# Two fused transformer blocks on one core: PSUM banks given by name, one projection and one bias product issued later, gathering by token tile, waits per half in the scattering

## The chip, the cores and the metric

One Trainium2 chip, one NeuronCore of it. The metric is the device time of one execution in microseconds. "The median" is that of three runs; the profile is of one execution more, whose own time stands beside it.

## What is computed

256 tokens of width 1024 go through two blocks. What the change touches of them, in the reference's own functions:

- Block one mixes latent attention (8 heads, 256 keys) and a Hyena convolution by spectra, then attends to a memory of 256 tokens, then runs a hierarchical mixture of experts. Beside the attention the kernel multiplies block two's conditioning vector with `w_ada_2` (6144 columns in twelve parts of 512, `ada0` to `ada11`).
- Block two normalises and modulates, runs a gated linear recurrence beside an attention with a relative bias (8 heads, causal), and a second mixture of experts.
- A mixture: each of the 256 tokens picks one group of four and two experts of eight in it, so 512 pairs of token and expert; `m = silu(t @ w_gate) * (t @ w_up)`, `y = m @ w_down`, weighted and summed per token. All 32 experts of a block are run.

## The kernel before

**PSUM.** There are eight banks of 128 x 512 float32. Every use of a bank is a stage in one long list (`STAGES`, lines 178 to 209). A stage without bank numbers takes the next banks in turn, a stage with a tuple takes those; lines 210 to 216 number the uses of each bank. `take` makes TensorE wait until the use before of the same bank was released by whoever reads it (`free`), `full` tells the readers that a stage's product is there, `ready` waits for a release. So the numbering decides which older reader a new product waits for.

**Order.** Each engine's program is written out by hand and runs in that order: TensorE (`block.tensor`), ScalarE (`block.scalar`), VectorE (`block.vector`), GpSimd (a few statistics and small loads), SyncE (all large loads, in order, each waiting until its ring slot is vacated). The ring has four slots of 3 MB; unit i goes into slot i mod 4 once unit i-4 is used up (`vacated`, by the table `LAST`). `occupy(stage, j, n)` (line 597) issues n matmuls of 256 columns into a bank that is free and about to be used; their product is overwritten.

**Block one's attention** (loop from line 839, one turn per head h): `ada(h+1)` (16 records of 32 x 512, line 752), transposing the probabilities (`pT`, 831), scores of head h+2 (824), `ada_col(h+1)` (763: one-column products that turn the row into columns), then the product with V (`pv`, 852). After head 2 comes `convolve(0)` (741, 742), after head 5 `z_spectrum(1)` (733), after head 7 `convolve(1)`. ScalarE copies out `ada` (1367) and `pT` (1440), takes the exponentials (1428) and issues the load of the memory tokens from its own queue at head 5 (1444); after the heads it converts weights (477) and squares the memory tokens (1294). VectorE takes the maxima (2007), adds the modulation (1905) and scales the heads (2023).

**A mixture, `moe(b)`** (from line 921): dummies, transposes (`rT`, 612), routing product (`rt`, 934), turned back (`rl`, 940); VectorE picks groups and experts in some 20 short steps; `cnt` (949 to 953) counts pairs by prefix sums; VectorE makes the 0/1 matrix `sel` (2183, 2184, one token tile after the other) and then the weighted one, `selw` (2196 to 2198), clears the tail (2204) and reads two positions into registers; `gx` (972) gathers the tokens for the 512 pairs, eight banks of two token tiles each in a high and a low part; ScalarE copies out the even banks (1566, 1568), VectorE the odd ones (2210, 2212) and then the first windows (2218); `swT` (980) transposes `selw`, VectorE makes it 0/1 (2224). Then come the 32 experts, one step each (997, 1004, 1011, 1017), on six banks counted from that of `yTa`. At the end `start_sum` (1075) opens four sums, `pairs_T` (1111) transposes the results of 64 rows into token form, ScalarE copies the high part (1627), VectorE the low part (2385), and `scatter` (1122, 1123) adds them by token.

In block one the bias product (`bias`, 958) stands between `cnt` and the gathering. It needs two small loads that GpSimd issues after `rt1` (2735, 2736). In block two `gate_row("g2r")` (918) stands there; it needs eight diagonals from ScalarE (1555). Both use the same tensor area as the transposed tokens.

**Block two's attention** (from line 1244): per head `aT` (1249), scores of h+2 (1164, 1165), `beside(h)`, the product with V (1261, 1262). `beside(0)` makes the sums of squares of the first token tile (1214), `beside(1)` those of the second, then the first quarter of an output projection (`wp_lru`). VectorE copies the sums at head 2 (2585) for GpSimd's root; VectorE uses that at head 3. Before it stand the projections `xl`, `aq`, `ak`, `yl`, `av` of the normalised tokens (627 to 629), with `g1r` (918) between `ak` and `yl`.

The stages' banks at the places that the prediction's steps touch, worked out from the list: `yl` takes 6 and 7, used last by `gx` (second) and `ak` (first); block one's experts use the banks from 3 on, block two's from 1 on.

## Time and profile before

| | |
|---|---|
| median of 3 runs | 1034.42 us (1033.56 to 1035.21) |
| the profiled execution, its own time | 1035.14 us |
| its span, first to last instruction | 1033.1 us |
| TensorE | 986.1 us busy (95%), 5320 matmul records |
| VectorE, ScalarE, GpSimd | 583.6, 352.2 and 21.1 us |
| mean granted TensorE clock | 0.988 of full speed |

The profiled execution takes 2.0 us more than its span, and 0.72 us more than the median. A TensorE record's duration overlaps with the next one's, so a busy share near one says that the engine was fed, not that it ran at its peak; the granted clock (1.0 is 2.4 GHz, 0.5 is 1.2 GHz) and what ended an idle stretch have to be read beside it. A float32 matmul leaves two records. "issue" as the releaser means that the profile shows nothing that was waited for; a semaphore of a bank can hide behind it.

### The profile page before, as it was taken

The numbers are of one execution on the slowest core, as the hardware profiler recorded it, in microseconds if no ns is written. First come the engines' busy times: TensorE is split into PE (matmuls) and PEld (weight loads), VectorE is DVE, ScalarE is ACT, GpSimd is POOL, SyncE is SP. The second block draws the span as 40 slices with busy tenths as digits, with TensorE's granted clock in tenths as the row PEclk, the third lists the DMA queues.
The fourth block names the chain that finished last, engine by engine and source line by source line (L and its number), as shares of the span: only waits on it lengthen the run. The fifth ranks groups of instructions, "written<-read, shape, count | busy, mean of one in ns | idle before, by whom it ended". The sixth has DMA issues, their size and how long they took to land.

```text
span 1033.1 us, 14969 instructions
## 1 busy us (share of the span) xinstructions
PE 986.1 (95%) x5320; PEld 593.7 (57%) x5320; DVE 583.6 (56%) x1110; ACT 352.2 (34%) x679; POOL 21.1 (2%) x41
## 2 busy tenths in 40 slices
PE   8999999999999899999999999999899999999985
PEld 7678566977967533443443479876763434434434
DVE  5834437555345546445445475678675655555556
ACT  5654324455445222222222354754441111111113
POOL 1000001000000000000000000000000000000000
PEclk9999999999999899999999999989999999999998
DMA  9263492446407499999999927350619999999931
GB/s 360 120 250 137 195 397 102 163 183 243 166 1 319 180 362 427 424 425 424 428 423 429 397 83 324 141 228 1 245 62 385 423 427 424 426 424 426 424 153 41
DMA packets 28895, 289.04 MB, mean 280 GB/s; under 512 B 3080, under 2 KB 5544, under 8 KB 7728
## 3 DMA queue, kind: packets, MB, share of 16 engines
q1 hardware_dynamic: 25344, 282.04, 66.4%
q0 software_dynamic: 1136, 3.74, 1.1%
q10 hardware_dynamic: 2368, 2.64, 0.8%
q8 instruction: 29, 0.48, 0.2%
q14 instruction: 18, 0.15, 0.0%
HBM read 287.34 MB, written 1.06 MB: 279 GB/s over the span
## 4 chain that ended last, share of the span: by engine, by line
PE 82%; DVE 9%; ACT 3%; DMA 3%; issue 2%; DVEq 0%; SPq 0%; POOL 0%; ACTq 0%; POOLq 0%
PE bank L997 23%; PE bank L1011 11%; PE bank L627 7%; PE bank L628 6%; PE bank L629 6%; PE bank L1017 6%; PE bank L1004 4%; DVE ring_r L484 2%; PE bank L720 2%; PE bank L752 2%; PE bank L972 1%; PE bank L733 1%; PE bank L604 1%; DMA ring<-in_lat 1%; DMA HT<-in_rel_bias 1%
## 5 line engine op out<-in xcount | busy, mean ns | idle before, releaser
L997 PE MATMUL bank<-ring,arena 128*64 128x512 f32 x1040 | 237.5, 598 | 0.2 <-DVE arena L2218 0.2
L2248 DVE TENSOR_REDUCE arena<-bank 128x512 f32 x130 | 83.7, 686 | 117.3 <-PE bank L1017 114.8
L484 DVE TENSOR_TENSOR ring_r<-ring,ring_r 128x1024 fp32r<-128x1024 f32 (+1 forms) x84 | 99.2, 1211 | 85.1 <-ACT ring_r L477 85.1
L997 PEld LDWEIGHTS bank<-ring,arena 128*64 128x64 f32 x1040 | 69.1, 136 | 122.7 <-issue 122.7
L1011 PE MATMUL bank<-ring,arena 128*64 128x512 f32 x520 | 125.8, 604 | 0.5 <-DVE arena L2263 0.3
L477 ACT ACTIVATE ring_r<-ring 128x1024 fp32r<-128x1024 f32 (+1 forms) x84 | 84.8, 1046 | 78.8 <-PE bank L629 77.2
L627 PE MATMUL bank<-HT_r,ring_r 128*128 128x256 f32 x352 | 101.2, 288 | 5.4 <-issue 2.1
L629 PE MATMUL bank<-HT_r,ring_r 128*128 128x256 f32 x352 | 99.6, 283 | 0.0
L1590 ACT ACTIVATE arena<-bank 128x512 f32<-128x512 f32 x64 | 38.3, 598 | 147.6 <-PE bank L997 147.6
L1017 PEld LDWEIGHTS bank<-tab,arena 128*128 128x128 f32 x520 | 55.7, 140 | 54.8 <-issue 49.6
L1017 PE MATMUL bank<-tab,arena 128*128 128x128 f32 x520 | 70.9, 279 | 3.3 <-DVE arena L2277 2.1
L627 PEld LDWEIGHTS bank<-HT_r,ring_r 128*128 128x128 f32 x352 | 67.3, 191 | 8.8 <-issue 8.7
L1584 ACT ACTIVATE arena<-arena 128x128 f32<-128x128 f32 x64 | 19.8, 309 | 152.6 <-DVE arena L2254 152.6
L629 PEld LDWEIGHTS bank<-HT_r,ring_r 128*128 128x128 f32 x352 | 67.4, 191 | 0.0
L628 PE MATMUL bank<-XN_r,ring_r 128*128 128x256 f32 x224 | 63.4, 283 | 0.0
L1011 PEld LDWEIGHTS bank<-ring,arena 128*64 128x64 f32 x520 | 31.7, 136 | 49.7 <-issue 48.3
L1004 PEld LDWEIGHTS bank<-tab,arena 128*128 128x128 f32 x260 | 27.2, 141 | 55.2 <-issue 50.3
L2254 DVE TENSOR_REDUCE arena<-bank 128x256 f32<-128x512 f32 x65 | 44.2, 681 | 12.9 <-PE bank L1004 12.9
L629 PE MATMUL bank<-ring_r,arena_r 128*128 128x512 f32 x128 | 50.6, 396 | 0.0
L2234 DVE COPY arena<-arena 128x512 f32 x62 | 26.5, 427 | 34.6 <-issue 34.6
L1004 PE MATMUL bank<-tab,arena 128*128 128x128 f32 x260 | 42.7, 287 | 2.2 <-ACT arena L1590 1.5
L1596 ACT ACTIVATE arena<-bank 128x512 f32<-128x512 f32 x32 | 19.1, 597 | 72.8 <-PE bank L1011 72.8
(436 smaller groups left out, 1431.5 us busy)
## 6 DMA issues: line engine op xcount, KB each, us to landing
ring<-in_experts SPq DMA_DIRECT2D x64, 2048.0 KB, 14.8
ring<-in_experts SPq DMA_DIRECT2D x64, 1024.0 KB, 11.1
ring<-in_ada SPq DMA_DIRECT2D x12, 2048.0 KB, 10.1
ring<-in_win SPq DMA_DIRECT2D x5, 2048.0 KB, 11.4
ring<-in_hy SPq DMA_DIRECT2D x3, 2048.0 KB, 19.5
ring<-in_mk SPq DMA_DIRECT2D x2, 2048.0 KB, 11.1
ring<-in_mv SPq DMA_DIRECT2D x2, 2048.0 KB, 10.5
ring<-in_wo SPq DMA_DIRECT2D x2, 2048.0 KB, 7.3
```

Of the source, the lines that this page charges most:

```text
L477: nc.scalar.activation(R(h), w, ACT.Copy).then_inc(sem("w_high"), 1)
L484: nc.vector.tensor_tensor(R(w), w, R(h), ALU.subtract).then_inc(sem("w_low"), 1)
L627: mm(ps, R(ah), R(bh), start=first, stop=False)
L628: mm(ps, R(ah), R(bl), start=False, stop=False)
L629: return mm(ps, R(al), R(bh), start=False, stop=last_)
L997: last = mm(gu_bank[g:g + WIN, :], xw[:, k, :], w[:, k * 512:(k + 1) * 512], start=k < 2, stop=k >= KD - 2)
L1004: last = tr(guT_bank[:, c * P:(c + 1) * P], gu_sb[:, c * P:(c + 1) * P], ident)
L1011: last = mm(d_bank[half][64 * f:64 * f + WIN, :], hb[:, f, :], w[:, o:o + 512], start=True, stop=True)
L1017: last = tr(dT_bank[c // 4][:, (c % 4) * P:(c % 4 + 1) * P], d_sb[:, c * P:(c + 1) * P], ident)
L1590: A_(gu_sb, gu_bank[:, :], ACT.Copy).then_inc(sem(f"gu_sb{b}"), 1)
L2248: last = V.reduce_sum(ysT[:, 4 * u:4 * u + 4, bass.ds(s, WIN)], dT_bank[u][:, :].rearrange("p (c g w) -> p c w g", c=4, g=2), AXX)
L2254: return V.reduce_sum(three(gu_sum, 4), guT_bank[:, :].rearrange("p (c g w) -> p c w g", c=4, g=2), AXX)
```

## The change

- **Order in block one's attention**: `ada(3)` moves from the head of turn 2 behind `convolve(0)`; `ada_col(3)`, ScalarE's copy and VectorE's addition for it move into turn 3. One dummy matmul stands between the two parts of `ada_col(1)`, one before the product with V in heads 6 and 7.
- **Banks by name** for both mixtures and the stages between them (`EXPERT`, `SUMS`, tuples). By the list `yl` takes 6 and 7 after `ga` (second) and `gx` (first); block one's experts use banks 5, 6, 7, 0, 1, 2, block two's 4, 5, 6, 7, 0, 1. `yTa1` now follows `gx1` and `bias` in its banks instead of `swT1`.
- **Block one's bias product** moves behind `swT1`, with ScalarE's copy and its small store behind the copies of `swT1`.
- **Gathering**: three banks first take both parts of token tile 0, then of tile 1, with a wait per tile; the other five run as before.
- **Block two's gate row** moves before the counts, its diagonals on ScalarE before the two exponentials; numbers of dummies change.
- **Scattering** waits for one half of 512 columns at a time and, but for the last part, runs by halves.
- **Block two's attention**: both token tiles' sums of squares move behind the first quarter of the projection in head 1; two dummies stand in head 0.

```diff
--- before.py
+++ after.py
@@ -189,16 +189,22 @@
 STAGES += [("ada8", 1), ("mo", 4), ("ada9", 1)]
 
 
+EXPERT = {1: (5, 6, 7, 0), 2: (4, 5, 6, 7)}
+SUMS = {1: (1, 2, 3, 4), 2: (0, 1, 2, 3)}
+
+
 def _moe_stages(b):
     one = b == 1
-    return [(f"rT{b}", 4)] + [("adac8", 1)] * one + [(f"rt{b}", 1), (f"rl{b}", 1, (3,))] + [("adac9", 1)] * one \
-        + [(f"cnt{b}", 1)] + [("bias", 1)] * one + [("g2r", 2, (5, 6))] * (b == 2) + [(f"gx{b}", 8), (f"swT{b}", 2, (3, 4))] \
-        + [(f"yTa{b}", 4), (f"sct{b}", 4), (f"yTb{b}", 4)]
+    return [(f"rT{b}", 4, *(() if one else ((3, 4, 5, 6),)))] + [("adac8", 1)] * one + [(f"rt{b}", 1), (f"rl{b}", 1, ((3,), (5,))[b - 1])] + [("adac9", 1)] * one \
+        + [(f"cnt{b}", 1)] + [("g2r", 2, (0, 1))] * (b == 2) + [(f"gx{b}", 8, ((3, 4, 5, 6, 7, 0, 1, 2), (4, 5, 6, 7, 0, 1, 2, 3))[b - 1])] \
+        + [(f"swT{b}", 2, ((3, 4), (6, 7))[b - 1])] + [("bias", 1, (0,))] * one \
+        + [(f"yTa{b}", 4, EXPERT[b]), (f"sct{b}", 4, SUMS[b]), (f"yTb{b}", 4, EXPERT[b])]
 
 
 STAGES += _moe_stages(1)
-STAGES += [("ada10", 1), ("ada11", 1)]
-STAGES += [("uT", 4), ("xl", 2), ("adac10", 1), ("adac11", 1), ("aq", 2), ("ga", 2), ("gx", 2), ("ak", 2), ("g1r", 2)]
+STAGES += [("ada10", 1, (1,)), ("ada11", 1, (2,))]
+STAGES += [("uT", 4, (3, 4, 5, 6)), ("xl", 2, (7, 0)), ("adac10", 1, (1,)), ("adac11", 1, (2,)), ("aq", 2, (3, 4)),
+           ("ga", 2, (5, 6)), ("gx", 2, (7, 0)), ("ak", 2, (1, 2)), ("g1r", 2, (3, 4))]
 STAGES += [("yl", 2, (6, 7)), ("av", 2, (4, 5)), ("as0", 1, (0,)), ("as1", 1, (1,))]
 for _h in range(H1):
     STAGES += [(f"aT{_h}", 1, (2,))] + ([(f"as{_h + 2}", 1, (_h % 2,))] if _h + 2 < H1 else [])
@@ -762,6 +768,8 @@
                     for c in range(4):
                         last = mm(ps[:, 4 * a + c:4 * a + c + 1], ada_sum(n)[:, c * P:(c + 1) * P], ones[:, 0:1],
                                   start=True, stop=True)
+                    if a + 1 < len(parts):
+                        mm(ps[:, 256:512], ident, T("iota")[:, 0:256], start=True, stop=True)
                 full(last, f"adac{i}")
 
             pe.wait_ge(sem("tab"), 32)
@@ -837,14 +845,18 @@
             for t in range(TT):
                 ready(pe, "uv", t)
             for h in range(H1):
-                if h < 6:
+                if h < 6 and h != 2:
                     ada(h + 1)
+                if h == 3:
+                    ada_col(3)
                 ready(pe, f"sc{h}")
                 probs_T(f"pT{h}", prob[:, h % 2])
                 if h + 2 < H1:
                     mla_scores(h + 2)
-                if h < 6:
+                if h < 6 and h != 2:
                     ada_col(h + 1)
+                if h >= 6:
+                    occupy(f"pv{h}", 0, 1)
                 ready(pe, f"pT{h}")
                 ps = take(pe, f"pv{h}")
                 for t in range(TT):
@@ -854,6 +866,7 @@
                 full(last, f"pv{h}")
                 if h == 2:
                     convolve(0)
+                    ada(3)
                 if h == 5:
                     z_spectrum(1)
             convolve(1)
@@ -920,7 +933,7 @@
 
             def moe(b):
                 if b == 2:
-                    occupy("rT2", 0, 17)
+                    occupy("rT2", 0, 18)
                 transposed(f"rT{b}", XN, KD, f"xn_r{b}")
                 if b == 1:
                     ada_col(8)
@@ -942,7 +955,9 @@
                 full(last, f"rl{b}")
                 if b == 1:
                     ada_col(9)
-                occupy(f"cnt{b}", 0, 10 if b == 2 else 8)
+                occupy(f"cnt{b}", 0, 6 if b == 2 else 8)
+                if b == 2:
+                    gate_row("g2r", diag2, "diag2")
 
                 pe.wait_ge(sem("hot"), b)
                 ps = take(pe, f"cnt{b}")
@@ -951,27 +966,26 @@
                 mm(ps[:, NE:2 * NE], ones, M12[:, 0, :], start=False, stop=True)
                 mm(ps[:, 2 * NE:3 * NE], ones, M12[:, 0, :], start=True, stop=False)
                 full(mm(ps[:, 2 * NE:3 * NE], ones, M12[:, 1, :], start=False, stop=True), f"cnt{b}")
-                if b == 1:
-                    pe.wait_ge(sem("onehot"), 32)
-                    pe.wait_ge(sem("mask_row"), 1)
-                    ps = take(pe, "bias")
-                    full(mm(ps[0:H1, :], relb[0:BUCKETS + 1, :], oneh[0:BUCKETS + 1, :], start=True, stop=True), "bias")
-
-                if b == 2:
-                    occupy("g2r", 0, 3)
-                    gate_row("g2r", diag2, "diag2")
-                occupy(f"gx{b}", 0, 4 if b == 2 else 6)
-
-                pe.wait_ge(sem(f"sel{b}"), TT)
-                pe.wait_ge(sem("xn_low"), TT * b)
-                for k in range(KD):
-                    ps = take(pe, f"gx{b}", k)
+                occupy(f"gx{b}", 0, 6)
+
+                def gather(k, t):
+
+                    for i, x in enumerate((xn_high, xn_low)):
+                        last = mm(gx[k][:, :], R(x[:, t, k * P:(k + 1) * P]), R(sel[:, t, :]),
+                                  start=t + i == 0, stop=t + i == TT)
+                    if t:
+                        full(last, f"gx{b}", k)
+
+                gx = [take(pe, f"gx{b}", k) for k in range(3)]
+                for t in range(TT):
+                    pe.wait_ge(sem(f"sel{b}"), t + 1)
+                    pe.wait_ge(sem("xn_low"), TT * (b - 1) + t + 1)
+                    for k in range(3):
+                        gather(k, t)
+                for k in range(3, KD):
+                    gx.append(take(pe, f"gx{b}", k))
                     for t in range(TT):
-
-                        for i, x in enumerate((xn_high, xn_low)):
-                            last = mm(ps[:, :], R(x[:, t, k * P:(k + 1) * P]), R(sel[:, t, :]),
-                                      start=t + i == 0, stop=t + i == TT)
-                    full(last, f"gx{b}", k)
+                        gather(k, t)
                 pe.wait_ge(sem(f"selw{b}"), TT)
                 for j in range(2):
                     ps = take(pe, f"swT{b}", j)
@@ -980,7 +994,12 @@
                             last = tr(ps[:, a * S + t * P:a * S + (t + 1) * P],
                                       selw[:, t, (2 * j + a) * P:(2 * j + a + 1) * P], ident)
                     full(last, f"swT{b}", j)
-                occupy(f"yTa{b}", 0, 2)
+                if b == 1:
+                    pe.wait_ge(sem("onehot"), 32)
+                    pe.wait_ge(sem("mask_row"), 1)
+                    ps = take(pe, "bias")
+                    full(mm(ps[0:H1, :], relb[0:BUCKETS + 1, :], oneh[0:BUCKETS + 1, :], start=True, stop=True), "bias")
+                occupy(f"yTa{b}", 0, 2 if b == 2 else 1)
                 for k in range(KD):
                     ready(pe, f"gx{b}", k)
                 if b == 2:
@@ -1040,6 +1059,8 @@
                         if isinstance(e, int) and e == 1:
                             for j in range(2):
                                 ready(pe, f"swT{b}", j)
+                            if b == 1:
+                                ready(pe, "bias")
 
                         before = 16 * (NE // RING) * (b - 1)
                         rounds = 16 * ((e - 1) // RING + 1) if isinstance(e, int) else \
@@ -1114,16 +1135,16 @@
                 def scatter(pt):
 
                     stage = (f"yTa{b}", f"yTb{b}")[pt // 2]
-                    for half in range(2):
+                    end = pt == NPAIR // P - 1
+                    for q in range(4):
+                        t, half = (q // 2, q % 2) if end else (q % 2, q // 2)
                         ready(pe, stage, 2 * (pt % 2) + half)
-                    for t in range(TT):
-                        for half in range(2):
-                            tok, cols = slice(t * P, (t + 1) * P), slice(half * 512, (half + 1) * 512)
-                            mm(acc[2 * t + half][:, :], R(swT[:, pt, tok]), R(ytok[:, pt, cols]), start=False, stop=False)
-                            last = mm(acc[2 * t + half][:, :], R(swT[:, pt, tok]), R(ytok_low[:, pt, cols]),
-                                      start=False, stop=pt == NPAIR // P - 1)
-                            if pt == NPAIR // P - 1:
-                                full(last, f"sct{b}", 2 * t + half)
+                        tok, cols = slice(t * P, (t + 1) * P), slice(half * 512, (half + 1) * 512)
+                        mm(acc[2 * t + half][:, :], R(swT[:, pt, tok]), R(ytok[:, pt, cols]), start=False, stop=False)
+                        last = mm(acc[2 * t + half][:, :], R(swT[:, pt, tok]), R(ytok_low[:, pt, cols]),
+                                  start=False, stop=end)
+                        if end:
+                            full(last, f"sct{b}", 2 * t + half)
 
                 pairs_T(f"yTa{b}", range(0, 4))
                 scatter(0)
@@ -1219,14 +1240,12 @@
             def beside(h):
 
                 if h == 0:
-                    pe.wait_ge(sem("squared"), 4)
-                    lss = take(pe, "lss")
-                    token_sums(lss, sq, range(4), (0,))
-                    wp_ps["lss"] = lss
+                    occupy("ap0", 0, 2)
                 elif h == 1:
-                    full(token_sums(wp_ps["lss"], sq, range(4), (1,)), "lss")
                     pe.wait_ge(sem("lo_low"), 1)
                     wp_lru(0, 0)
+                    pe.wait_ge(sem("squared"), 4)
+                    full(token_sums(take(pe, "lss"), sq, range(4)), "lss")
                 elif h == 2:
                     wp_lru(0, 1)
                 elif h in (4, 5):
@@ -1432,7 +1451,9 @@
             mla_exp(0)
             mla_exp(1)
             for h in range(H1):
-                if h < 6:
+                if h == 3:
+                    ada_evac(3)
+                if h < 6 and h != 2:
                     ada_evac(h + 1)
                 ps = got(act, f"pT{h}")
                 if h >= 2:
@@ -1546,20 +1567,16 @@
                 ps = got(act, f"rt{b}")
                 free(A_(turned, ps[:, 0:S], ACT.Copy), f"rt{b}")
                 A_(R(xn_high[:, 1, :]), XN[:, 1, :], ACT.Copy).then_inc(sem("xn_high"), 1)
+                if b == 2:
+                    for k in range(KD):
+                        last = A_(diag2[:, k, :], ident, ACT.Copy, scale=mod[:, 40 + k:41 + k])
+                    last.then_inc(sem("diag2"), 1)
                 act.wait_ge(sem("e_diff"), b)
                 A_(ex2, m2, ACT.Exp).then_inc(sem("e_exp"), 1)
                 act.wait_ge(sem("g_diff"), b)
                 A_(gex, cand4, ACT.Exp).then_inc(sem("g_exp"), 1)
                 if b == 2:
-                    for k in range(KD):
-                        last = A_(diag2[:, k, :], ident, ACT.Copy, scale=mod[:, 40 + k:41 + k])
-                    last.then_inc(sem("diag2"), 1)
                     copies("g2r", [g2row[:, 0:512], g2row[:, 512:1024]])
-                if b == 1:
-                    ps = got(act, "bias")
-                    free(A_(brow[0:H1, :], ps[0:H1, :], ACT.Copy), "bias")
-                    ready(act, "bias")
-                    act.dma_start(bias_rows, brow[0:H1, :]).then_inc(sem("bias_out"), 16)
                 for k in range(0, KD, 2):
                     ps = got(act, f"gx{b}", k)
                     if shift is None:
@@ -1574,6 +1591,11 @@
                                   accum_out=pair_w[:, 2 * j + a:2 * j + a + 1])
                     last.then_inc(sem("x_high"), 1)
 
+                if b == 1:
+                    ps = got(act, "bias")
+                    free(A_(brow[0:H1, :], ps[0:H1, :], ACT.Copy), "bias")
+                    ready(act, "bias")
+                    act.dma_start(bias_rows, brow[0:H1, :]).then_inc(sem("bias_out"), 16)
                 for j in range(2):
                     ready(act, f"swT{b}", j)
                 gu_bank, guT_bank, d_bank, dT_bank = expert_banks(b)
@@ -2017,7 +2039,9 @@
                     mla_max(h + 2)
                 ready(dve, f"sc{h}")
                 link(V.reciprocal(rinv[:, h, :], rsum[:, h, :]))
-                if h < 6:
+                if h == 3:
+                    modulation(3)
+                if h < 6 and h != 2:
                     modulation(h + 1)
                 ps = got(dve, f"pv{h}")
                 free(V.tensor_tensor(AO[:, :, h * VD:(h + 1) * VD], three(ps[:, 0:TT * VD], TT),
```

## Rows read from the trace of the kernel before

**Rows 1.** The page: the chain that ended last, by engine, and the expert loop's costliest group.
```profile
PE 82%; DVE 9%; ACT 3%; DMA 3%; issue 2%; DVEq 0%; SPq 0%; POOL 0%; ACTq 0%; POOLq 0%
...
L997 PE MATMUL bank<-ring,arena 128*64 128x512 f32 x1040 | 237.5, 598 | 0.2 <-DVE arena L2218 0.2
```

**Rows 2.** Timeline of TensorE in block one's attention: start us, us, engine, line, operation, count.
```profile
123.73 2.89 PE L752 MATMUL bank<-ring,cm 128*32 128x512 f32 x16 [1.89 <-DMA ring<-in_ada]
...
130.31 1.08 PE L741 MATMUL bank<-arena 128*128 128x512 f32 x2
...
142.36 1.92 PE L752 MATMUL bank<-ring,cm 128*32 128x512 f32 x16
...
147.40 1.92 PE L752 MATMUL bank<-ring,cm 128*32 128x512 f32 x16
```

**Rows 3.** Timeline of ScalarE and VectorE beside it, heads three to seven.
```profile
141.60 0.16 DVE L1905 TENSOR_TENSOR mod<-bank,col 128x4 f32<-128x4 f32 x1
...
164.54 1.06 ACT L1294 ACTIVATE arena<-XN 128x1024 f32<-128x1024 f32 x1
```

**Rows 4.** DMA queues, 150 to 160 us: ScalarE's queue, and that load's time to landing.
```profile
q10 hardware_dynamic: 131, 0.54, 13.9%
...
XN<-in_mem ACTq DMA_DIRECT2D x1, 1024.0 KB, 12.8
```

**Rows 5.** Timeline of TensorE from block one's counts to its first expert.
```profile
339.22 1.54 PE L958 MATMUL bank<-HT 33*8 33x512 f32 x2 [2.54 <-DMA HT<-in_rel_bias]
...
345.61 8.01 PE L972 MATMUL bank<-arena_r 128*128 128x512 f32 x32
...
356.06 1.13 PE L604 MATMUL bank<-tab 128*128 128x256 f32 x4 [1.57 <-DVE arena_r L2224]
357.12 3.65 PE L997 MATMUL bank<-ring,arena 128*64 128x512 f32 x16
```

**Rows 6.** Stretches: length, TensorE busy (instructions), granted clock, DMA share, GB/s.
```profile
339.22:345.61 6.39, 6.39 (x14) 0.53 1.00 424
...
686.25:695.41 9.16, 9.16 (x33) 0.63 0.67 284
```

**Rows 7.** Timeline of VectorE after block one's counts.
```profile
339.31 0.75 DVE L2184 SCALAR_TENSOR_TENSOR arena_r<-tab,arena,arena_r 128x512 fp32r<-128x512 f32 x1
...
346.30 0.48 DVE L2204 MEMSET arena<- 128x512 f32 x1
```

**Rows 8.** The same stage in block two: VectorE, and TensorE's first expert.
```profile
763.04 0.48 DVE L2204 MEMSET arena<- 128x512 f32 x1 [0.17 <-DVE arena L2198]
...
764.20 2.97 DVE L2212 TENSOR_SCALAR arena<-bank,mod 128x512 f32<-128x512 f32 x4 [0.67 <-issue]
...
768.09 3.65 PE L997 MATMUL bank<-ring,arena 128*64 128x512 f32 x16 [0.21 <-DVE arena L2218]
```

**Rows 9.** Timeline of the scattering, block one (block two shows the same pattern).
```profile
589.65 2.73 DVE L2385 SCALAR_TENSOR_TENSOR arena_r<-bank,arena,arena_r 128x512 fp32r<-128x512 f32 x4 [1.77 <-ACT arena_r L1627]
591.21 0.47 PE L1122 MATMUL bank<-arena_r 128*128 128x512 f32 x1 [1.14 <-DVE arena_r L2385]
```

**Rows 10.** Timeline at the start of the stage `yl`: VectorE and TensorE.
```profile
656.48 1.41 DVE L1824 COPY arena<-bank 128x256 f32<-128x256 f32 x4
...
657.33 0.36 PE L627 MATMUL bank<-HT_r,ring_r 128*128 128x256 f32 x1 [1.88 <-issue]
```

**Rows 11.** Timeline of TensorE in block two's attention, heads zero and one.
```profile
685.30 1.02 PE L1214 MATMUL bank<-tab,arena 128*128 128x1 f32 x8 [0.71 <-ACT arena L1360]
...
695.41 0.65 PE L1261 MATMUL bank<-arena 128*64 128x256 f32 x2
```

**Rows 12.** Timeline of block two's routing: ScalarE's copies and TensorE's dummies.
```profile
732.49 7.50 PE L604 MATMUL bank<-tab 128*128 128x256 f32 x34
...
746.60 1.05 ACT L1548 ACTIVATE arena_r<-XN 128x1024 fp32r<-128x1024 f32 x1
...
752.65 2.43 ACT L1555 ACTIVATE HT<-tab,mod 128x128 f32<-128x128 f32 x8
```

## The prediction

> **What bounds the kernel now.** I read the chain of waits first. TensorE carries 82% of it, VectorE 9% [rows 1], so a microsecond counts only where TensorE stands still, runs at its lower clock, or does something it need not. Then I asked of the largest stage, the 64 expert steps, whether there is anything to gain or lose: over 1040 records TensorE was idle 0.2 us in all before them [rows 1]. The experts' loop is fed without a hole, and its instructions stay as they are. What can move is the seams between stages. For each seam that the diff touches I read TensorE's timeline (its idle time and what ended it), the granted clock of the stretch behind it, and the timelines of ScalarE and VectorE beside it, because the seam is worth only what the next-latest engine leaves of it.
>
> **The change part by part.** Negative is faster.
>
> *Block one's heads.* After head 1 TensorE waits 1.89 us for the weights of `ada(3)`, up to 123.73 [rows 2]; head 2 therefore runs from 121.84 to 130.31, where `convolve(0)` starts: 8.47 us. An undisturbed turn with the same work takes 147.40 - 142.36 = 5.04 us [rows 2]. The difference, 3.43 us, is the wait and the lower clock behind it (the record group behind the wait takes 2.89 us against 1.92 for the same 16 records [rows 2]). Once `ada(3)` stands behind `convolve(0)`, some 7 us later, its weights have long landed. Added: a dummy in `ada_col(1)`. 17 dummies take 7.50 us [rows 12], so one takes 0.44 and two 0.88; this one lies on TensorE's path: +0.44. The later `ada_col(3)` shares its bank with `pv3`, and VectorE frees that only after head 5's maximum: its addition takes 0.16 us at 141.60 in the turn shown [rows 3], right behind the maximum, while TensorE would go on with `pv` at once; I put the wait at the addition and the reciprocal before it, two steps of 0.16 and their hand-over: +0.4 (none at best, 0.6 at worst). The dummies of heads 6 and 7 stand between a transpose and the product that needs ScalarE's copy of it, a gap that hides 0.44; uncovered they would cost 0.9 together. TensorE thus saves 2.6 us.
> But the next stage starts from VectorE, which needs the memory tokens' squares, and ScalarE begins those at 164.54 [rows 3], just when the load lands: issued at head 5, it takes 12.8 us to land [rows 4]. If the load's time stays, it lands 2.6 us earlier with its issue; if the bytes before it set its end, hardly at all. By 160 us its queue had moved only 0.54 MB of 1.05 [rows 4], so both limits play a part. The ends are -2.6 and -0.5; I take -1.9, nearer to the first because the row is a transfer that advanced beside the others all the time. The later `ada_col(3)` also holds back the next large load on SyncE's queue by some 6 us, behind two others under way: hidden, or 1 us if not.
> The Trainium skill ("DMA: Bandwidth & Descriptors", section on queues, rings and completion order) says that each DMA engine takes turns packet by packet between the queues that have work. Taken alone that gives the load a share from its issue on, and so the whole -2.6; the 0.54 MB agree that it got one.
>
> *Block one's bias product and gathering.* The counts end 2.54 us before 339.22, at 336.68; TensorE then waits for the small load of the bias, and the six dummies and the bias behind it run at a granted 0.53 until 345.61, where the gathering starts [rows 5, 6]. VectorE had the first tile's `sel` at 339.31 + 0.75 = 340.06 [rows 7]. After: dummies 336.7 to 339.3, an idle 0.8 us, gathering from 340.1; its 32 records take at most the 8.0 us of before [rows 5] and end by 348.1. By token tile, TensorE works six records on the first tile, 1.5 us, until the second tile is there at 341.3.
> What is late next is VectorE. It is busy with `selw` up to its memset at 346.30, unchanged [rows 7]. From there I take block two's rows: evacuation 1.16 us after the memset began, four of them in 2.97 us, the first expert 3.89 us after the first evacuation began [rows 8]. So 346.30 + 1.16 + 3.89 = 351.35. Against 357.12 [rows 5]: -5.8. TensorE has to be ready by then: `swT1` needs a bank of the first odd evacuation (348.2), the bias one of the third (347.5 + 3 x 0.74 = 349.7); with the bias at 0.8 us and one dummy it is done at 351.0, with the bias at its 1.54 us of the lower clock [rows 5] at 351.7. That bounds the term at -5.4. Before, the dummies waited 1.57 us for VectorE's copy of `swT1` [rows 5]; by the new banks nothing waits for it before the first step's end. The bias's store on ScalarE's queue, 0.6 us of copy and as much of issue, now delays nothing but ScalarE's first copy of an expert, which is due only after 16 records of 3.65 us.
>
> *Block two's gathering.* The same edits find VectorE already last: it begins its evacuations 1.16 us after the memset whatever TensorE does, and the first expert waits for it [rows 8]. The gate row moves into the time of the four dummies taken from before the counts; its diagonals (2.43 us) can start at 746.60 + 1.05 [rows 12] and end at 750.1, the two products at 751.9, the counts are due at 752.4. So 0. If the diagonals were late the counts would be: up to 1 us. The 18th dummy before the transposes stands where VectorE's normalisation is last; uncovered, 0.44.
>
> *Scattering.* Before the first `scatter` TensorE waits 1.14 us for VectorE's second half; one low part takes 2.73 / 4 = 0.68 us [rows 9]. Waiting for the first half only saves that 0.7. The last part follows VectorE as closely, and I put 0.2 on it, an estimate (none at least, another 0.7 at most): -0.9 in each block, -1.8 in all.
>
> *Banks before `yl`.* TensorE stands 1.88 us before `yl` with no releaser named; VectorE's copies of `ak` begin at 656.48, and 0.7 us later the first of its banks is free, when `yl` starts at 657.33 [rows 10]. With banks 6 and 7 after `ga` and `gx`, both read by ScalarE long before, nothing holds it: -1.9. The converted weights behind it follow TensorE's own use, so they move along.
>
> *Block two's heads 0 and 1.* Before: 0.71 us idle, then 0.95 us of one-column products up to 686.25 [rows 11]; the stretch from there to head 1's product with V at 695.41 takes 9.16 us at a mean granted clock of 0.63 [rows 6, 11]. At full clock the same records take 9.16 x 0.63 = 5.8 us: -3.4. The idle time and first sums are replaced by two dummies (0.88 us instead of 1.66: -0.8), and those sums come back in head 1 (+0.95). Together -3.2 if the clock stays up, +0.2 if it does not. VectorE reads the sums only at head 2. I take -3.2: the idle time that preceded the fall is filled.
>
> **Sum:** -1.9 - 5.8 + 0 - 1.8 - 1.9 - 3.2 = -14.6. The profiled execution, 1035.1 us, becomes 1020.5; it lies 0.7 above the median, so the median of 1034.4 becomes 1019.8.
>
> **Rivals.**
> *The clock falls all the same.* In the two seams where it fell before, idle stretches of 0.8 to 1.0 us and one-column products remain, now side by side with others. Against: 1.57 us idle before 356.06 [rows 5] were followed by none, as the next 16 records took the 3.65 us that they take in block two [rows 5, 8]. In block two's heads that costs 3.4, before block one's experts up to 0.4 by TensorE's readiness and up to 1 more by a late eighth bank: 1023.2 to 1024.6. Chance 0.2.
> *The memory load is bound by bytes.* The first term shrinks to -0.5: 1021.2. For: half of it was outstanding at 160. By the page's rule of turns it would not be. Chance 0.12.
> *VectorE's chain takes over in block two's heads.* It is 56% busy over the span, has a dozen short steps in each head, and then of the 3.2 only the part before head 1 stays, 0.8: 1022.2. Against: the lower clock held TensorE, not VectorE, which so has time in hand [rows 6]. Chance 0.06.
> *The banks are not what held `yl`.* The profile names no releaser [rows 10]; if it was the converted weights, the change does nothing there: 1021.7. Chance 0.03.
> *Slower: the experts' banks.* If the new pairing of the six banks lengthened each of the 64 steps, 0.23 us a step would eat all 14.6; at 0.3 us, half a record, it is 64 x 0.3 = 19.2 on 1019.8, so 1039.0. Against: the two blocks use different banks already and TensorE is held 0.2 us in both together [rows 1]. Chance 0.02.
>
> **The numbers.** All terms as summed: 0.57, at 1019.8, by itself 1017.5 to 1021.5. The range must take in the clock and the load, alone and together, and below it terms that I bounded from above (the hole of 1 us that dummies leave): 1015.5 to 1025.5. About 0.2% of this kernel's time, 2 us, is what a measurement can tell from no change. For that 12.6 us of the sum would have to fail: faster 0.96, the same 0.02, slower 0.02.
>
> **What the profile after would show.** `ada(3)` behind `convolve(0)` with no DMA named before it, head 2 in about 5 us or less, clock 1.0; the squares of the memory at 162 to 164. The gathering about 3.5 us after the counts, 0.8 to 1 us idle before it, block one's first expert 5.0 to 5.2 us after the memset. No idle time before `yl`. Clock 1.0 through heads 0 and 1. First `scatter` 0.5 us after its transposes. The same length of an expert's step as before, in both blocks. Wrong would be: an expert step of another length, a stretch at 0.5 in one of the seams, or VectorE or a DMA named before the stage behind a seam with the same idle time as before.

## The result, and the profile after

The changed kernel took 1020.77 us (median of four runs, 1019.63 to 1022.08), the kernel before 1034.58 beside it (1033.56 to 1035.21): a ratio of 0.9868, 95% interval [0.9851, 0.9885]. The forecast was 1019.8, in a range from 1015.5 to 1025.5. The profiled execution has a span of 1017.6 us against 1033.1, 15.5 less; the medians differ by 13.8. That gap of 1.7 us turned out to be the most instructive part of the case, below.

The timeline of TensorE in block one's attention, after (columns as in [rows 2]):

```profile
122.06 0.61 PE L839 MATMUL bank<-tab,arena 128*128 128x128 f32 x4
...
124.30 1.08 PE L747 MATMUL bank<-arena 128*128 128x512 f32 x2
...
131.32 3.64 PE L758 MATMUL bank<-ring,cm 128*32 128x512 f32 x32
...
138.44 1.08 PE L864 MATMUL bank<-arena 128*128 128x64 f32 x8 [0.36 <-DVE mod L1927]
...
149.43 1.08 PE L739 MATMUL bank<-arena 128*128 128x512 f32 x2
```

Head 2 begins with its transposes and no wait, and `convolve(0)` starts at 124.30 instead of 130.31. `ada(3)` and `ada(4)` stand together behind it, 32 records without a wait. The only new wait is 0.36 us for VectorE's addition, in the bank that `ada_col(3)` shares with `pv3`. `z_spectrum(1)` starts at 149.43, before at 152.35. The memory tokens' load takes 13.0 us, and the stage behind it moves along (the timelines of ScalarE and TensorE):

```profile
161.81 1.06 ACT L1313 ACTIVATE arena<-XN 128x1024 f32<-128x1024 f32 x1
...
172.82 0.36 PE L633 MATMUL bank<-HT_r,ring_r 128*128 128x256 f32 x1 [1.01 <-DVE arena_r L1870]
```

The squares start 2.73 us earlier than in [rows 3]. ScalarE's own weight conversion in front of them ended at about the same moment in both kernels (at 164.63 before, at 161.71 after), so the load was not the only thing that they could have waited for. The large loads ahead of that one moved as well (SyncE's queue, issues):

```profile
143.64 5.37 SPq L539 DMA_DIRECT2D ring<-in_mv x2
```

The first of these two was issued at 146.56 before. The seam before block one's experts, against [rows 5]:

```profile
333.74 2.84 PE L610 MATMUL bank<-tab 128*128 128x256 f32 x12
337.54 7.54 PE L974 MATMUL bank<-arena_r 128*128 128x512 f32 x32 [0.97 <-DVE arena_r L2208]
344.92 0.60 PE L994 MATMUL bank<-tab,arena 128*128 128x128 f32 x4
345.67 0.66 PE L994 MATMUL bank<-tab,arena 128*128 128x128 f32 x4
347.08 1.01 PE L1001 MATMUL bank<-HT 33*8 33x512 f32 x2 [0.74 <-DVE arena L2234]
348.02 0.70 PE L610 MATMUL bank<-tab 128*128 128x256 f32 x2
348.65 3.65 PE L1016 MATMUL bank<-ring,arena 128*64 128x512 f32 x16
```

The wait of 2.54 us for the bias's input is gone, the 12 records of dummies take 2.84 us instead of 5.49, and the gathering starts 3.8 us after the counts' end. VectorE's memset is at 343.52 and the first expert 5.13 us behind it. In block two, against [rows 8], VectorE is again what the first expert waits for:

```profile
751.80 1.03 PE L610 MATMUL bank<-tab 128*128 128x256 f32 x4
753.64 0.65 PE L1016 MATMUL bank<-ring,arena 128*64 128x512 f32 x2 [0.81 <-DVE arena L2242]
```

TensorE stands 0.81 us there where it stood 0.21 before, and the first expert comes 14.45 us earlier than before, as much as the counts ahead of it (14.49). The start of scattering and of `yl`, against [rows 9, 10]:

```profile
582.25 0.50 PE L1143 MATMUL bank<-arena_r 128*128 128x512 f32 x1 [0.40 <-DVE arena_r L2409]
```

```profile
644.29 1.88 PE L931 MATMUL bank<-arena,tab 128*128 128x512 f32 x4
645.61 0.68 PE L633 MATMUL bank<-HT_r,ring_r 128*128 128x256 f32 x1
```

`yl`'s first record now follows the gate row with no idle time. And block two's heads 0 and 1, against [rows 11]:

```profile
673.13 1.13 PE L610 MATMUL bank<-tab 128*128 128x256 f32 x4
674.19 0.65 PE L1280 MATMUL bank<-arena 128*64 128x256 f32 x2
...
679.16 1.84 PE L1235 MATMUL bank<-tab,arena 128*128 128x1 f32 x16
680.93 0.65 PE L1280 MATMUL bank<-arena 128*64 128x256 f32 x2
```

Their stretch, with its granted clock (third number after the length: PEclk), against [rows 6]:

```profile
674.19:680.93 6.74, 6.74 (x40) 5.41 (x39) 4.67 (x11) 3.80 (x10) 0.00 (x0) 1.00 0.99 421
```

6.74 us at full clock in place of 9.16 at 0.63. The experts' group has the same duration as in [rows 1], to the digit:

```profile
L1016 PE MATMUL bank<-ring,arena 128*64 128x512 f32 x1040 | 237.5, 598 | 1.0 <-DVE arena L2242 0.8
```

**One table for all that follows.** I took the same ten landmarks of TensorE from the profiled execution of every kernel. A column is the length of a stretch, in us, and below the first line the difference from the changed kernel. A: start to `z_spectrum(1)`. B: to block one's counts. C: to its first expert. D: its experts, to `start_sum`. E: scattering, to `xl`. F: to block two's first transposed probabilities. G: to head 1's product with V. H: to the transposes for block two's routing. I: to its first expert. K: to the end.

| kernel | A | B | C | D | E | F | G | H | I | K | span |
|---|---|---|---|---|---|---|---|---|---|---|---|
| changed | 149.43 | 183.17 | 16.05 | 226.45 | 27.41 | 69.35 | 9.07 | 45.58 | 27.13 | 263.96 | 1017.6 |
| before | +2.92 | -0.14 | +5.69 | -0.26 | +1.09 | +2.09 | +3.09 | +0.01 | -0.04 | +1.05 | 1033.1 |
| u1 | +1.65 | +0.20 | +0.02 | -0.27 | +0.03 | -0.01 | 0.00 | +3.16 | -0.02 | +0.04 | 1022.4 |
| u2 | +0.23 | +0.12 | +3.80 | -0.27 | +0.07 | +0.02 | 0.00 | +0.03 | -0.03 | +0.23 | 1021.8 |
| u3 | +0.19 | +0.11 | +0.02 | -0.27 | -0.01 | -0.01 | 0.00 | +1.59 | -0.03 | +0.01 | 1019.2 |
| u4 | +0.19 | -0.01 | +0.01 | -0.27 | +0.07 | +3.12 | 0.00 | +1.55 | -0.03 | -0.03 | 1022.2 |
| u5 | +2.09 | +0.10 | +0.02 | -0.27 | +0.01 | -0.01 | +4.46 | +0.13 | -0.04 | +0.01 | 1024.1 |
| u6 | +2.80 | -0.08 | +0.02 | -0.27 | -0.01 | +0.03 | -0.21 | +3.11 | -0.02 | +0.03 | 1023.0 |
| u9 | +1.76 | +0.11 | +0.02 | -0.27 | -0.01 | +0.02 | -0.01 | 0.00 | -0.03 | +0.01 | 1019.2 |
| u7 | -0.14 | +0.09 | +0.02 | +1.41 | +1.10 | 0.00 | 0.00 | +0.02 | -0.04 | +1.14 | 1021.2 |
| u10 | +1.83 | +0.18 | +0.34 | -0.26 | +0.02 | 0.00 | 0.00 | +0.06 | -0.03 | -0.04 | 1019.7 |
| u8 | -0.29 | +0.19 | +0.02 | -0.26 | -0.01 | +0.01 | 0.00 | +0.05 | -0.04 | +0.03 | 1017.3 |
| n1 | +0.15 | +0.37 | -1.18 | -0.27 | +0.03 | +0.03 | 0.00 | +0.03 | -1.47 | +0.01 | 1015.3 |
| n3 | +0.10 | +0.69 | -1.21 | -0.27 | +0.02 | 0.00 | 0.00 | +1.57 | -1.45 | +0.05 | 1017.1 |

Most cells from C on that no edit touches agree within 0.1 us, those of A and B within some 0.3, so a seam can be read to a tenth or three where the total can't: the four or five runs of one kernel spread over 1 to 4 us. The ratios below carry little of the argument: of the twelve variants only n1 and n3 have an interval that lies clear of the changed kernel's, and the ten from u1 to u10 overlap with it. So what a part is worth rests on the traces, one execution of each kernel. The record adds the mean clock of every timed run, to 0.001, which is about 1 us of lost clock on this kernel; the four of the changed kernel have 0.996 or 0.997. The cells that are large without an edit (A of u1, u5, u6, u9, u10; D of u7; H of u1, u3, u4, u6, n3) are a finding of their own, told last; B of n1 and n3 is the memory tokens' load, which landed later there. D is 0.27 longer in the changed kernel than in all others, before included: block one's last expert waited 0.20 us for its weights in that one execution.

```profile
564.63 0.65 PE L1016 MATMUL bank<-ring,arena 128*64 128x512 f32 x2 [0.20 <-DMA ring<-in_experts]
```

### The profile page after: what moved, and what is told of

The parts are those of the page before. It is cut to its first block and busy times, and to the rows that moved or that the text cites. A ratio compares the mean times of both kernels' runs of the same rounds, so it can differ in the third digit from the quotient of the medians.

```text
span 1017.6 us, 14965 instructions
## 1 busy us (share of the span) xinstructions
PE 978.0 (96%) x5320; PEld 588.6 (58%) x5320; DVE 583.0 (57%) x1110; ACT 352.4 (35%) x679; POOL 21.1 (2%) x41
## 3 DMA queue, kind: packets, MB, share of 16 engines
HBM read 287.34 MB, written 1.06 MB: 283 GB/s over the span
```

## The experiments

All twelve start from the changed kernel. Those of one group ran on one chip beside the kernel before, and each ratio is to that.

### Group one: the parts put back one by one (before: 1035.37 us)

**u1.** Back in head 2: `ada(3)`, its copy on ScalarE and its addition on VectorE.
```
-                if h < 6 and h != 2:
+                if h < 6:
                     ada(h + 1)
-                if h == 3:
-                    ada_col(3)
...
                     convolve(0)
-                    ada(3)
...
```


> The changed kernel with ada(3), its copy and its addition back at head 2, all else as changed. Theory: TensorE waits about 1.9 us for the weights of ada(3) again, its clock falls behind the wait, head 2 takes some 8.5 us up to convolve(0) instead of 5.1, and mk starts about 2.7 us later: 1023.5 (1022.7 if the wait comes back but the clock stays up). Rival, that the gain there came from the dummies: no change, 1020.8. Second rival, that the memory load's end is set by the bytes before it: the load, issued about 2.9 us later, lands at nearly the same time, and the total is 1021.3 or less.

1022.38 us (1021.05 to 1024.37), ratio 0.9866 [0.9849, 0.9883]. No wait for weights came back; something else stood in its place:

```profile
117.38 3.61 PE L758 MATMUL bank<-ring,cm 128*32 128x512 f32 x16
...
124.10 1.92 PE L758 MATMUL bank<-ring,cm 128*32 128x512 f32 x16
...
129.04 1.08 PE L747 MATMUL bank<-arena 128*128 128x512 f32 x2
```

```profile
117.38:124.10 6.72, 6.72 (x42) 0.75 0.98 380
```

In head 1, with no idle time ahead of them, the 16 records of `ada(2)` took 3.61 us instead of 1.92, at a mean clock of 0.75. TensorE thus came to `ada(3)` at 124.10, after the moment at which it had been released in [rows 2] (123.73), and found its weights. The slow stretch and the wait are substitutes: the 1.65 us in A is the slow stretch (the same records are 1.5 to 1.7 us longer in three other kernels), and the order itself cost nothing in this execution. So the gain of part one depends on what head 1 did: in the profiled pair 2.9 us, here none. None of the three expectations named this mechanism, though the ratio, 0.9866 against 0.9868, is the one that the first rival (no change) gives. The median is 1.6 above that of the changed kernel, in another comparison and inside the spread. One timed run had a clock of 0.997, as high as the changed kernel's best, and a span of 1019.1 us against 1017.6 and 1018.0 there: a cost of 1.1 to 1.5 us without the lower clock, as the wait would make; that run has no trace.

**u2.** The bias product in front of the gathering again, in bank 2, with ScalarE's copy and store; two dummies stand before the first expert again instead of one.
```
+                if b == 1:
+                    pe.wait_ge(sem("onehot"), 32)
+                    pe.wait_ge(sem("mask_row"), 1)
+                    ps = take(pe, "bias")
+                    full(mm(ps[0:H1, :], relb[0:BUCKETS + 1, :], oneh[0:BUCKETS + 1, :], start=True, stop=True), "bias")
                 occupy(f"gx{b}", 0, 6)
...
-                occupy(f"yTa{b}", 0, 2 if b == 2 else 1)
+                occupy(f"yTa{b}", 0, 2)
...
```


> The changed kernel with block one's bias product (and ScalarE's copy and store of it) back in front of the gathering, which stays by token tile. Theory: the product's late input and the lower clock behind it come back, block one's first expert starts 5.5 to 5.8 us later, 1026.4. Rival, that gathering by token tile brought part of it: only 4.5 us or less come back, 1025.3 or less. Block two is untouched under both.

1022.97 us (1021.92 to 1023.91), ratio 0.9873 [0.9855, 0.9891].

```profile
336.70 1.64 PE L973 MATMUL bank<-HT 33*8 33x512 f32 x2 [2.44 <-DMA HT<-in_rel_bias]
338.27 5.49 PE L610 MATMUL bank<-tab 128*128 128x256 f32 x12
343.20 7.90 PE L979 MATMUL bank<-arena_r 128*128 128x512 f32 x32
350.93 1.03 PE L999 MATMUL bank<-tab,arena 128*128 128x128 f32 x8
351.80 1.03 PE L610 MATMUL bank<-tab 128*128 128x256 f32 x4
352.80 1.08 PE L1016 MATMUL bank<-ring,arena 128*64 128x512 f32 x4
```

Wait and lower clock came back in full: the gathering starts 5.31 us later relative to the counts. But the first expert does so by 3.80 only. The other 1.9 of the 5.69 us lay behind the gathering before. There the dummies waited 1.57 us for the bank of the turned weights, with VectorE's copy of them named as releaser [rows 5]; u2, with the named banks, has no such wait. From the start of VectorE's last evacuation to the first expert it is 3.46 us before and 1.67 in u2, while from the gathering's start to that evacuation it is 8.05 and 7.93. So the order of gathering can be worth 0.1 of it and the banks the rest, and the rival had the size and not the reason. No run puts the old banks back by themselves.

**u3.** The gathering slice by slice, each waiting for both token tiles.
```
-                gx = [take(pe, f"gx{b}", k) for k in range(3)]
-                for t in range(TT):
-                    pe.wait_ge(sem(f"sel{b}"), t + 1)
...
-                    for k in range(3):
-                        gather(k, t)
-                for k in range(3, KD):
+                gx = []
+                pe.wait_ge(sem(f"sel{b}"), TT)
...
+                for k in range(KD):
...
```


> The changed kernel with the gathering slice by slice, each waiting for both token tiles, in both blocks. Theory, VectorE's evacuations set the first expert: gathering starts 1.2 us later, but the first expert only 0.7 us later in block one (the bias product still has to fit in) and 0 to 0.2 in block two: 1021.6. Rival, that TensorE sets it: 1.2 us in each block, 1023.2. Second rival, wholly hidden: 1020.8.

1021.37 us (1020.94 to 1022.23), ratio 0.9862 [0.9845, 0.9879]. The gathering starts 1.0 us later in both blocks, and both first experts are where they were: 0.02 and -0.03 in C and I.

```profile
338.83 7.55 PE L974 MATMUL bank<-arena_r 128*128 128x512 f32 x32 [1.96 <-DVE arena_r L2205]
...
347.39 1.01 PE L998 MATMUL bank<-HT 33*8 33x512 f32 x2
```

The bias product had waited 0.74 us for a bank; now it does not. Gathering by token tile is worth nothing here.

**u4.** `ak` in the two banks that `yl` takes next.
```
-           ("ga", 2, (5, 6)), ("gx", 2, (7, 0)), ("ak", 2, (1, 2)), ("g1r", 2, (3, 4))]
+           ("ga", 2, (5, 6)), ("gx", 2, (7, 0)), ("ak", 2, (6, 7)), ("g1r", 2, (3, 4))]
```


> The changed kernel with ak's products in banks 6 and 7, which yl takes right behind them, all other banks as changed. Theory, banks held yl: TensorE stands about 1.9 us before yl again until VectorE has read ak's first bank, and the end is 2.1 us later, 1022.9. Rival, that the wait was for the converted weights: no idle time, 1020.8.

1024.71 us (1024.23 to 1025.84), ratio 0.9896 [0.9879, 0.9913].

```profile
649.05 0.36 PE L633 MATMUL bank<-HT_r,ring_r 128*128 128x256 f32 x1 [2.55 <-DVE arena L1846]
```

The wait is back, and here the profile names its releaser, VectorE's copies of `ak`. It is longer than the 1.88 us of [rows 10], and F is 3.12 us longer instead of 2.1. Banks held `yl`: shown. The ratio's interval still overlaps with the changed kernel's, but every run of u4 (1024.23 and more) is slower than every run of that (up to 1022.08).

### Group two: block two's heads, and scattering (before: 1034.14 us)

**u5.** The first tile's sums in head 0 instead of the dummies, the second's in head 1, as before the change.
```
                 if h == 0:
-                    occupy("ap0", 0, 2)
+                    pe.wait_ge(sem("squared"), 4)
+                    lss = take(pe, "lss")
+                    token_sums(lss, sq, range(4), (0,))
...
                 elif h == 1:
+                    full(token_sums(wp_ps["lss"], sq, range(4), (1,)), "lss")
...
-                    full(token_sums(take(pe, "lss"), sq, range(4)), "lss")
```


> The changed kernel with the sums of the squares back in heads 0 and 1 of block two and without the two dummies of head 0. Theory: about 0.7 us of idle time and 0.95 us of one-column products come back, the clock falls behind them, and the stretch up to head 1's product with V takes about 9.2 us at a mean of 0.6: 3.2 us later, 1024.0. Rival, the clock has nothing to do with it: 0.2 us, 1021.0.

1024.64 us (1024.43 to 1026.12), ratio 0.9898 [0.9868, 0.9927]. The rows of the seam, and its clock:

```profile
675.85 1.02 PE L1235 MATMUL bank<-tab,arena 128*128 128x1 f32 x8 [0.71 <-ACT arena L1381]
676.80 0.65 PE L1282 MATMUL bank<-arena 128*64 128x256 f32 x2
...
680.20 1.86 PE L1235 MATMUL bank<-tab,arena 128*128 128x1 f32 x8
```

```profile
676.80:687.33 10.53, 10.53 (x33) 0.53 0.59 249
```

4.46 us, 1.4 more than in the kernel before: the lower level began earlier (the transposes at 677.79 already take 0.90 instead of 0.55) and lasted through the stretch. All four timed runs have a clock of 0.991 or 0.992.

**u6.** Only the two dummies left out.
```
                 if h == 0:
-                    occupy("ap0", 0, 2)
+                    pass
```


> The changed kernel without the two dummies of head 0 (the sums stay in head 1). Theory A, idle time makes the clock fall: 1.6 us of idle before the first product with V, then the lower clock, about 3 us later, 1023.8. Theory B, it was the one-column products that made it fall: the clock stays at 1.0, nothing is later, 1020.8.

1022.15 us (1020.67 to 1024.99), ratio 0.9869 [0.9837, 0.9901].

```profile
676.48 0.62 PE L1280 MATMUL bank<-arena 128*64 128x256 f32 x2 [0.80 <-ACT arena L1379]
```

```profile
676.48:683.21 6.73, 6.73 (x40) 1.00 0.96 408
683.21:691.29 8.08, 8.08 (x24) 0.59 0.05 19
```

TensorE stood 0.80 us idle, half of what I had expected but more than the 0.71 before the change, and the clock stayed up through heads 0 and 1: theory A falls for an idle time of this length, and the dummies buy nothing there (G is even 0.21 shorter). But in head 2, behind the 16 records of one-column products that now end head 1, the clock fell: 3.11 us in H.

**u9.** Both: the two dummies, and behind them the sums as in u5.
```
                 if h == 0:
                     occupy("ap0", 0, 2)
+                    pe.wait_ge(sem("squared"), 4)
+                    lss = take(pe, "lss")
+                    token_sums(lss, sq, range(4), (0,))
...
```


> The changed kernel with two dummies in head 0 and behind them the sums of the first token tile, those of the second in head 1 as before. Theory A (idle time decides): the clock stays at 1.0, head 0 is up to 0.9 us longer and head 1 some 0.9 us shorter, 1020.9. Theory B (one-column products decide): the clock falls, 1023.9.

1021.29 us (1019.52 to 1021.67), ratio 0.9860 [0.9829, 0.9891]. Clock 1.0 from 676.61 to 682.55, G unchanged. So theory B doesn't hold alone either. Of four arrangements only idle time and one-column products together, as before the change and in u5, brought the lower clock inside this seam; either of the change's two edits would have kept it out in these executions. Each arrangement has one trace, but the timed runs agree: clocks of 0.995 to 0.997 in u9, and 0.995 or 0.996 in three of u6's four, against u5's 0.991 and 0.992.

**u7.** Each `scatter` waits for both halves and goes by token tile.
```
-                    for q in range(4):
-                        t, half = (q // 2, q % 2) if end else (q % 2, q // 2)
-                        ready(pe, stage, 2 * (pt % 2) + half)
+                    for half in range(2):
+                        ready(pe, stage, 2 * (pt % 2) + half)
+                    for q in range(4):
+                        t, half = q // 2, q % 2
```


> The changed kernel with each scatter waiting for both halves and taking token tile by token tile, in both blocks. Theory: the wait before the first scatter grows from 0.4 to 1.1 us, and the last part is some 0.4 us later: 1.1 us in each block, 1022.9. Rival, only the first scatter counts: 0.7 in each, 1022.2.

1023.57 us (1022.07 to 1024.40), ratio 0.9887 [0.9856, 0.9918]. The first part waits as in [rows 9]:

```profile
584.37 0.47 PE L1144 MATMUL bank<-arena_r 128*128 128x512 f32 x1 [1.15 <-DVE arena_r L2410]
```

E and K are 1.10 and 1.14 longer: 0.74 and 0.75 at the first part, 0.36 and 0.39 at the last. The theory's 1.1 a block is shown.

### Group three: dummies, and a better version (before: 1034.89 us)

**u10.** No dummies before block one's gathering.
```
-                occupy(f"gx{b}", 0, 6)
+                occupy(f"gx{b}", 0, 6 if b == 2 else 0)
```


> The changed kernel without the six dummies before block one's gathering: TensorE stands about 3.8 us there instead of 1. Theory: the clock falls and the gathering runs part of its time at the lower level, 2 to 4 us of which VectorE does not hide: 1023 to 1025. Rival, the clock stays up or the fall is hidden behind VectorE: 1020.8.

1021.56 us (1020.13 to 1021.95), ratio 0.9864 [0.9848, 0.9879].

```profile
339.55 9.07 PE L974 MATMUL bank<-arena_r 128*128 128x512 f32 x32 [3.64 <-DVE arena_r L2208]
348.46 1.03 PE L994 MATMUL bank<-tab,arena 128*128 128x128 f32 x8
```

The clock did fall: the same 32 records take 9.07 us instead of 7.54. Of these 1.53 us only 0.34 reach the first expert; VectorE's evacuations hide the rest. The theory had the fall right and the uncovered part wrong.

**u8.** Without the dummies in `ada_col(1)` and in heads 6 and 7.
```
-                    if a + 1 < len(parts):
-                        mm(ps[:, 256:512], ident, T("iota")[:, 0:256], start=True, stop=True)
...
-                if h >= 6:
-                    occupy(f"pv{h}", 0, 1)
```


> The changed kernel without the dummy in ada_col(1) and those of block one's heads 6 and 7. Theory: the first costs its own 0.4 us and buys nothing, the others lie in a wait for ScalarE: 0.4 us earlier, 1020.4, clock unchanged. Rival, they keep the clock up: a stretch at the lower level behind head 1 or in heads 6 and 7, 1 to 2 us later, 1022.3.

1022.32 us (1019.28 to 1023.58), ratio 0.9879 [0.9862, 0.9896]. A is 0.29 shorter than in the changed kernel and about 0.5 shorter than in u2 to u4; the clock stayed up in this profiled execution, whose span of 1017.3 is below the changed kernel's. But it was the exception. The other three timed runs have clocks of 0.994, 0.992 and 0.993, below all four of the changed kernel, and spans of 1019.3 to 1021.6 us, and the median is the rival's number (1022.3). This speaks for the rival, that the dummies make a fall of the clock rarer; where those three runs lost their clock no trace shows, and the interval overlaps with the changed kernel's, so it is not shown.

**n1.** ScalarE evacuates six gathered slices as TensorE completes them, VectorE two.
```
-                for k in range(0, KD, 2):
+                for k in (0, 1, 2, 3, 4, 6):
...
-                for k in range(1, KD, 2):
+                for k in (5, 7):
```


> The changed kernel with ScalarE evacuating six of the eight gathered slices as TensorE completes them (0 to 4 and 6) and VectorE only slices 5 and 7, in both blocks. Theory, VectorE's four evacuations are what is last before the first expert: it starts 1.2 us earlier in block one and 1.5 in block two, 1018.1. Rival, TensorE's transposes and the bias product are nearly as late: half of that, 1019.5. Second rival, block one's experts wait for their weights at the loop's end by as much as they start earlier: 1019.3.

1017.49 us (1016.70 to 1018.89), ratio 0.9832 [0.9819, 0.9846]: faster than both kernels, since the interval lies below the changed kernel's [0.9851, 0.9885] against the same kernel before. The theory's 1.2 and 1.5 us measured 1.18 and 1.47.

```profile
345.39 1.41 DVE L2234 TENSOR_SCALAR arena<-bank,col 128x512 f32<-128x512 f32 x2 [0.87 <-issue]
```

```profile
345.44 1.03 PE L994 MATMUL bank<-tab,arena 128*128 128x128 f32 x8
346.40 1.02 PE L1001 MATMUL bank<-HT 33*8 33x512 f32 x2
347.36 0.70 PE L610 MATMUL bank<-tab 128*128 128x256 f32 x2
347.99 1.51 PE L1016 MATMUL bank<-ring,arena 128*64 128x512 f32 x6
```

TensorE now runs from the gathering into the experts with no hole.

**n3.** The edits of n1 (not shown again), and the memory tokens' load issued ahead of head 7's exponentials.
```
+                if h + 2 == H1 - 1:
+                    got(act, f"sc{h + 2}")
+                    act.dma_start(XN, A["mem"].rearrange("(t p) d -> p t d", p=P)).then_inc(sem("mem_in"), 16)
                 if h + 2 < H1:
                     mla_exp(h + 2)
-                if h + 2 == H1 - 1:
-                    act.dma_start(XN, A["mem"].rearrange("(t p) d -> p t d", p=P)).then_inc(sem("mem_in"), 16)
```


> The same, and ScalarE issues the memory tokens' load as soon as head 7's scores are done (the last reader of the buffer), ahead of the exponentials instead of behind them. Theory, the load takes the same 13 us from its issue: its squares and mk start 0.9 us earlier, 1017.2. Rival, the bytes before it set its end, or convolve(1) becomes the last: mk moves less than 0.3 us, 1018.0.

1018.19 us (1017.46 to 1019.89), ratio 0.9834 [0.9821, 0.9847]. The load was issued at 148.00 instead of 148.94 in n1, took 14.5 us instead of 13.3, and its squares began no earlier (n3's timeline, then n1's):

```profile
162.54 1.06 ACT L1313 ACTIVATE arena<-XN 128x1024 f32<-128x1024 f32 x1 [0.72 <-DMA XN<-in_mem]
```

```profile
162.28 1.06 ACT L1313 ACTIVATE arena<-XN 128x1024 f32<-128x1024 f32 x1 [0.42 <-DMA XN<-in_mem]
```

B is 0.32 longer than in n1, as the later squares make it. An earlier issue of this one load was worth nothing in this execution. It could not have been worth the 0.9 us that I expected either: ScalarE was converting weights until 161.86 in n1 and waited only 0.42 us for the load.

## Why the prediction was right, and where it was not

**Block one's heads.** The step failed in size, and its rival in its premise. TensorE gained 2.92 us where I had 2.6 (dummy and bank wait measured 0.4 and 0.36 against 0.44 and 0.4; the rest is inside the spread of A). I took 1.9 for the end, a third of the way to "bound by bytes"; it was 2.74. What I had not seen: the loads ahead of the memory tokens' are issued as TensorE releases buffers, so they moved with it (`mv` by 2.92 us), and the whole group kept its shape. I had also not named ScalarE's weight conversion, which ends just when the load lands and so caps what an earlier landing can give. n3 shows the other side. Moved alone, the load did not land earlier, which speaks for other transfers setting its end (one execution each, and n1's squares already came 0.3 us later after `z_spectrum(1)` than the changed kernel's with no edit there). The Trainium skill ("DMA: Bandwidth & Descriptors", section on queues, rings and completion order) says that each DMA engine takes turns packet by packet between the queues that have work. Taken alone that would have given this load an earlier landing with an earlier issue; n3 does not show one (0.94 us earlier at the issue, 0.26 us later at the squares). And u1 shows that the gain is not there in every execution.

**Block one's bias product and gathering.** -5.8 expected, -5.69 measured, the first expert 5.13 us after the memset. By parts: the product's place 3.8 (u2, at most 0.4 of it the second dummy), the banks of the turned weights most of the rest (argued from the releaser named in [rows 5] and its absence in u2), the order of gathering 0 in the changed kernel (u3). That VectorE comes next is shown by n1.

**Block two's gathering.** 0 expected, -0.04 seen in I.

**Scattering.** -0.9 a block expected; 1.09 and 1.05 measured. The estimate of 0.2 for the last part measured 0.36 and 0.39 (u7).

**Banks before `yl`.** -1.9 expected, 2.09 measured; u4 brings the wait back with VectorE named.

**Block two's heads.** -3.2 expected, 3.09 measured, and the reason was half right; that the number came out so well is in part luck. I took the dummies to be what keeps the clock up, by filling the idle time. u6 leaves them out and u9 moves the sums back behind them, and in both the clock stays up. The rival "the clock falls all the same" did not happen in the profiled execution, but the case that I priced with it happens one head later, in some executions.

**The total.** The terms as measured give 15.5 us, 0.9 more than the sum, and the median 13.8, 0.8 less. So errors of both signs met: the heads of block one, the scattering and `yl` gave 1.4 us more than their terms, and the spread between executions took back 1.7. The prediction had no term for executions that differ from the profiled one.

**The unnamed term.** In the thirteen profiled executions of the changed kernel and its variants, stretches of the lower clock appear that no edit explains: 1.5 to 1.7 us in head 1 of block one, behind `ada_col(1)`'s 16 records of one-column products and `pv`, in four (u1, u5, u9, u10); 1.6 or 3.1 us in head 2 of block two, behind the 16 records of one-column sums, in five (u1, u3, u4, u6, n3); 1.7 us in u7's first expert of block one, behind a wait of 0.75 us, where the changed kernel waited 0.74 and lost nothing; 2.8 us in the first 120 us of u6, most of it behind a wait of 3.41 us for a load at its start. Together some 22 us over thirteen executions, 1.7 on average. The changed kernel's own profile has none of them, and is its fastest run, 1.1 below its median. The gap between 15.5 and 13.8 is this 1.1 and the 0.6 by which the profiled execution of the kernel before lies above its own median. The stretches are large enough for the first part, as an average. The clocks of the timed runs bear it out: the changed kernel's four have spans of 1017.6 and 1018.0 us at 0.997, and of 1019.2 and 1019.6 at 0.996. The second part was not looked into; the 23 timed runs of the kernel before in the three groups have clocks from 0.985 to 0.991, so it varies as well. Of head 2's, the moved sums are the plausible cause (before, they stood in heads 0 and 1, and H of the kernel before has no such stretch), but only one execution of the kernel before was read; that the sums in their new place cause them was not tested by taking them away.

## What to carry to other kernels

Price a seam by the engine that is next-latest, and then look at what that engine is made of: n1's 2.65 us lay in handing two of VectorE's four evacuations to an idle ScalarE. A wait and a stretch of lower clock ahead of it can stand for each other, so a part's worth read from one profile can be too high. Compare landmarks of profiled executions stretch by stretch before comparing medians: a few tenths of a microsecond show there, where medians blur two; and look at the clock of every timed run, since one profiled execution can be the lucky one (u8).

## What the runs showed of the hardware

- The granted clock can fall to its lower level with no idle time ahead: in u1, 16 records of 3.61 us instead of 1.92 behind one-column products. Whether it does differs between executions of the same instructions: block one's heads are the same in u9 and u10, where it fell, and in u3 and u4, where it did not.
- 0.80 us idle (u6) and 8 records of one-column products behind dummies (u9) left the clock at 1.0 through that seam; 0.71 us idle and 8 such records together were followed by a mean of 0.53 over 10.5 us (u5).
- 3.64 us idle before the gathering (u10) cost 1.53 us of lower clock; about 1 us idle there cost none: the same records took 7.50 to 7.55 us in ten profiles.
- A load issued 0.94 us earlier, with the DMA engines' busy share at 0.84 to 1.06 up to 160 us, took 1.2 us longer (14.5 against 13.3 us).
